# Combining the experts' outputs by adding DMAs while the last two experts run

## What is computed

```python
g_sel = argmax(g_logits); g_w = softmax(g_logits)[g_sel]
top_val, top_idx = top_k(expert logits of that group, 2)
top_w = softmax(top_val) * g_w
hid = silu(xs @ w_gate[e]) * (xs @ w_up[e])          # 1024 -> 512, per expert
x = x + sum over the 2 chosen e of top_w * (hid @ w_down[e])
```

## Time and profile before

| what | value |
|---|---|
| median of 3 runs | 1806.68 us (1804.47 to 1806.95) |
| the profiled execution | 1805.12 us |
| its span, first to last instruction | 1803.3 us |
| granted TensorE clock, mean | 0.991 |
| DMA moved | 241.31 MB |

### The profile page before, as it was taken

How to read it: one execution, slowest core, us unless ns; L and a number is a source line. 1 busy time by engine, 2 the same in 40 slices (tenths; PEclk the granted TensorE clock), 3 DMA queues, 4 the chain that set the end, 5 groups by cost and what they waited for, 6 DMA issues and landing times.

```text
span 1803.3 us, 25340 instructions
## 1 busy us (share of the span) xinstructions
PE 1745.9 (97%) x10151; PEld 1436.3 (80%) x10151; DVE 1184.1 (66%) x1701; ACT 888.6 (49%) x1413; POOL 349.9 (19%) x228
## 2 busy tenths in 40 slices
PE   9999999999999999999999999999999989999993
PEld 7998788999897677788999866765568868888882
DVE  6666645554466655555776588586764466988896
ACT  5525434234334544334344455556552366878781
POOL 4333222001242322001000276310010030000001
PEclk9999999999999999999999999999999999999997
DMA  6203112223312212333222210213243449999984
GB/s 191 77 25 100 47 48 72 93 71 117 97 59 67 65 39 71 101 94 99 94 94 72 70 48 24 71 47 95 69 151 118 142 172 394 414 407 416 398 349 175
DMA packets 121903, 241.31 MB, mean 134 GB/s; under 512 B 9577, under 2 KB 101258, under 8 KB 115642
## 3 DMA queue, kind: packets, MB, share of 16 engines
q1 hardware_dynamic: 113770, 212.81, 33.4%
q0 software_dynamic: 4464, 16.25, 2.4%
q10 hardware_dynamic: 3552, 10.62, 1.5%
HBM read 223.41 MB, written 16.25 MB: 133 GB/s over the span
## 4 chain that ended last, share of the span: by engine, by line
PE 51%; DVE 5%; ACT 4%; issue 1%; DMA 1%; POOL 0%; POOLq 0%; ACTq 0%; DVEq 0%
PE acc L1451 15%; PE acc L900 10%; PE acc L1166 9%; PE acc L1191 7%; PE acc L1255 2%; PE acc L1269 2%; PE acc L1286 1%; PE acc L1277 1%; PE acc L1151 1%; PE acc L1435 1%; DVE upad L2890 1%; DVE qk L2890 1%; ACT v L2087 1%; DMA qk<-y_rows,back_rows 0%; PE acc L1073 0%
## 5 line engine op out<-in xcount | busy, mean ns | idle before, releaser
L900 PE MATMUL acc<-h_split,ring_split 128*128 128x264 f32 (+1 forms) x864 | 269.4, 312 | 0.0
L900 PEld LDWEIGHTS acc<-h_split,ring_split 128*128 128x128 f32 x864 | 162.3, 188 | 9.7
L1191 PE MATMUL acc<-ring_split,h_split 128*128 128x256 f32 x384 | 107.9, 281 | 0.0
L900 PE MATMUL acc<-h_split,qk_split 128*128 128x264 f32 (+1 forms) x288 | 92.7, 322 | 1.3 <-DVE ring_split L2346 1.3
L900 PE MATMUL acc<-ring_split,qk_split 128*128 128x264 f32 (+1 forms) x288 | 92.2, 320 | 0.0
L3206 POOL TENSOR_TENSOR latent<-latent 128x528 f32<-128x528 f32 x18 | 29.1, 1619 | 285.7 <-ACT latent L1615 285.4
L2346 DVE TENSOR_TENSOR ring_split<-ring,qk_split 128x1024 fp32r<-128x1024 f32 (+1 forms) x56 | 59.4, 1070 | 34.1 <-ACT qk_split L1620 34.1
L900 PE MATMUL acc<-h_split,krope_split 128*128 128x264 f32 (+1 forms) x240 | 79.4, 331 | 1.9 <-POOL ring_split L3220 1.9
L3220 POOL TENSOR_TENSOR ring_split<-ring,krope_split 128x1024 fp32r<-128x1024 f32 x20 | 48.1, 2405 | 152.3 <-ACT krope_split L1620 152.3
L900 PE MATMUL acc<-ring_split,krope_split 128*128 128x264 f32 (+1 forms) x240 | 77.0, 321 | 0.0
L2346 DVE TENSOR_TENSOR ring_split<-ring,o_split 128x1024 fp32r<-128x1024 f32 (+1 forms) x32 | 43.9, 1389 | 49.3 <-ACT o_split L1620 49.1
(11 more groups left out here) (604 smaller groups left out, 5578.8 us busy)
## 6 DMA issues: line engine op xcount, KB each, us to landing
ring<-in_w_in SPq DMA_DIRECT2D x64, 1024.0 KB, 5.3
ring<-in_w_expert_gate SPq DMA_DIRECT2D x10, 2048.0 KB, 11.0
ring<-in_w_expert_up SPq DMA_DIRECT2D x10, 2048.0 KB, 9.9
ring<-in_w_expert_down SPq DMA_DIRECT2D x10, 2048.0 KB, 10.6
ring<-in_w_out SPq DMA_DIRECT2D x12, 1024.0 KB, 5.5
y_rows<-gate ACTq DMA_DIRECT2D x16, 512.0 KB, 10.4
hres<-in_w_expert_up SPq DMA_DIRECT2D x3, 2048.0 KB, 10.5
qk<-in_w_expert_down SPq DMA_DIRECT2D x3, 2048.0 KB, 11.0
```

The lines of the kernel that those rows point to most:

```text
L900: ins = nc.tensor.matmul(dst[0:rows_, half, 0:x.shape[1]], w[:, k, :], x, start=(k == 0 and i == 0), stop=(k == last and i == 2), skip_gro ...
L1191: ins = nc.tensor.matmul(dst[:, side, 0:WIDE], x[k][:, rows_], w, start=(k == 0 and part == 0), stop=(k == DC - 1 and part == 2), skip_gro ...
```

## The change

- **Weights in the eviction.** PE makes the weight of each expert's 128 slots (`slot_weights`: 8 small matmuls in iteration 0), and ACT's eviction of `y` multiplies by it as its scale. Rows of a token's two experts then only have to be added.
- **Adding gathers.** POOL gathers rows of `y_rows` with an adding DMA straight into `x_tok`: step 0 four tiles of the lower choice, after expert 13's rows are stored; step 1 four tiles of the other choice, after expert 14's. Where a token's lower choice is expert 14 the two are swapped. A token of expert 15 or past the 128 rows gets a row of zeros instead. DVE's eight multiply-adds fall away, and SP stores each tile when its two gathers have landed. The row numbers are made in the expert loop on DVE (`places_of_all`, `rows_fetched`, at e = 1 and e = 5).
- **Expert 15** is not stored in `y_rows`. Its down product is made by column halves (all of columns 0 to 511, then 512 to 1023), each evicted by itself, and POOL adds each half's 128 rows of 2 KB to `out` in HBM by an adding scatter, after the stores of `out`. Its tokens' numbers come from a pick on DVE, 4 small matmuls on PE (`rows_added`, e = 4) and two small steps on DVE.
- **Order of the last experts.** down(14) goes ahead of up(15): PE runs half of gate(15), turns the hidden part of 14, the other half of gate(15), down(14), up(15), hidden part and down of 15. ACT and DVE follow; on DVE the last weight half comes behind `hidden_low(15)`. The last three outputs have SBUF places of their own (`y_at`).
- **Overflow.** An overflow tile is weighted and added to `out` by a scatter. One block of zeros is stored instead of seven. POOL reaches the overflow count when both scatters have landed.

```diff
+ADDED = 1
+FETCHED = EXPERTS - ADDED
...
+        y_at = [y_out] * (EXPERTS - 3) + [x_gath[0], y_out, x_gath[1]]
...
-            granules += [("gate", e + 1), ("up", e + 1), ("down", e)]
+            granules += [("gate", e + 1)] + [("up", e + 1), ("down", e)][::1 if e < EXPERTS - 2 else -1]
...
+            for i in range(QT):
+                sp.wait_ge(rows_back[i], 32)
+                sp.dma_start(out[0, i * P:(i + 1) * P, :], x_tok[:, i, :]).then_inc(stored, 16)
...
+            def last_out_of_hidden(e):
+                i = granule_no["down", e]
+                hu, hl = (t.rearrange("p (k s) -> p k s", k=HID // P) for t in (ht_up, ht_low))
+                for side in range(2):
+                    n_ = slice(side * 512, side * 512 + 512)
+                    for half in range(2):
+                        pe.wait_ge(w_low_made, 2 * i + half + 1)
+                        wu, wl = granule_half(i, half, "up"), granule_half(i, half, "low")
+                        for k in range(HID // P // 2):
+                            c = half * HID // P // 2 + k
+                            ins = three(TWO["y"][:, side, :], hu[:, c, :], hl[:, c, :], wu[:, k, n_], wl[:, k, n_],
+                                        c == 0, c == HID // P - 1)
+                    done(ins, ("y_side", side) if side == 0 else ("y", e))
...
-            for e in range(EXPERTS - 1):
+            for e in range(EXPERTS - 2):
                 gate_of(e + 1)
                 hidden_of(e)
                 into_hidden("up", e + 1)
-                if e + 2 < EXPERTS:
-                    turn_expert(e + 2)
+                turn_expert(e + 2)
+                if e == 0:
+                    slot_weights()
+                if e == 4:
+                    rows_added()
                 down_of(e)
+            gate_of(EXPERTS - 1, range(1))
+            hidden_of(EXPERTS - 2)
+            into_hidden("gate", EXPERTS - 1, range(1, 2))
+            down_of(EXPERTS - 2)
+            into_hidden("up", EXPERTS - 1)
             hidden_of(EXPERTS - 1)
...
+            def last_out(side, label):
+                act.wait_ge(psum_filled, at(psum_filled, label))
+                e, n_ = EXPERTS - 1, slice(side * 512, side * 512 + 512)
+                evacuated(nc.scalar.activation(y_at[e][:, n_], acc[:, 2, side, :], ACT.Copy,
+                                               scale=R[:, R_WS + e:R_WS + e + 1]), label)
+
             def expert_out(e):
                 act.wait_ge(psum_filled, at(psum_filled, ("y", e)))
-                if e:
+                if e == 0:
+                    act.wait_ge(dve_made, at(dve_made, "slot_weights"))
+                elif e < EXPERTS - 3:
                     act.wait_ge(y_main, 16 * e)
-                evacuated(nc.scalar.activation(y_out, acc[:, 2, :, :].rearrange("p a b -> p (a b)"), ACT.Copy),
-                          ("y", e))
+                elif e == EXPERTS - 2:
+                    act.wait_ge(y_main, 16 * (EXPERTS - 3))
+                evacuated(nc.scalar.activation(y_at[e], acc[:, 2, :, :].rearrange("p a b -> p (a b)"), ACT.Copy,
+                                               scale=R[:, R_WS + e:R_WS + e + 1]), ("y", e))
                 act.wait_ge(act_evacuated, at(act_evacuated, ("y", e)))
-                act.dma_start(y_rows[e * P:(e + 1) * P, :], y_out).then_inc(y_main, 16)
+                act.dma_start(y_rows[e * P:(e + 1) * P, :], y_at[e])\
+                    .then_inc(y_main if e < EXPERTS - 3 else y_late[e - (EXPERTS - 3)], 16)
...
+            j = 2 * granule_no["gate", EXPERTS - 1]
+            expert_out(EXPERTS - 3)
+            weights_up(j + 2)
+            hidden_up(EXPERTS - 2)
+            weights_up(j + 3)
+            expert_gated(EXPERTS - 1)
+            weights_up(j + 4)
+            weights_up(j + 5)
+            expert_out(EXPERTS - 2)
+            weights_up(j + 6)
+            weights_up(j + 7)
             hidden_up(EXPERTS - 1)
-            expert_out(EXPERTS - 2)
-            expert_out(EXPERTS - 1)
-            act.sem_inc(y_stored, 1)
-            mark(y_stored)
-            act.wait_ge(y_main, 16 * EXPERTS)
+            last_out(0, ("y_side", 0))
+            last_out(1, ("y", EXPERTS - 1))
...
+            made(tt(r(R_BY, 2, 64), r(R_SEL[0], 2, 64), R[:, R_W:R_W + 64].unsqueeze(1).to_broadcast([P, 2, 64]), ALU.mult),
+                 "by_choice")
...
+            def rows_fetched():
+
+                base, ok, row = (R[:, x:x + 8] for x in (R_S, R_S + 8, R_WT))
+                own, slot = late(K_TOKEN, 1), R[:, R_SLOT:R_SLOT + 8]
+                first = late(K_FIRST, 16).unsqueeze(1).to_broadcast([P, 8, 16])
+                chain(tt(r(R_KEY, 8, 16), r(R_SEL[0], 8, 16), first, ALU.mult))
+                chain(nc.vector.tensor_reduce(base, r(R_KEY, 8, 16), AX.X, ALU.add))
+                chain(ts(ok, slot, float(P), None, ALU.is_lt))
+                chain(stt(out=ok, in0=base, scalar=float(FETCHED * P), in1=ok, op0=ALU.is_lt, op1=ALU.mult))
+                chain(stt(out=row, in0=base, scalar=-float(FETCHED * P + 1), in1=slot, op0=ALU.add, op1=ALU.add))
+                chain(ts(row, row, own, None, ALU.subtract))
+                chain(tt(row, row, ok, ALU.mult))
+                chain(ts(row, row, own, float(FETCHED * P), ALU.add, ALU.add))
+                swap, higher, lower = R[:, R_S + 8:R_S + 12], row[:, 0:4], row[:, 4:8]
+                chain(ts(swap, base[:, 4:8], float((EXPERTS - 2) * P + 1), None, ALU.is_equal))
+                chain(tt(R[:, R_S + 12:R_S + 16], lower, higher, ALU.subtract))
+                chain(tt(swap, swap, R[:, R_S + 12:R_S + 16], ALU.mult))
+                chain(tt(higher, higher, swap, ALU.add))
+                chain(tt(lower, lower, swap, ALU.subtract))
+                made(nc.vector.tensor_copy(back_rows[:, :], row), "back_rows")
...
+                if e == 0:
+                    slot_weights()
+                elif e == 1:
+                    places_of_all()
+                elif e - 2 < ADDED:
+                    added_pick(e - 2)
+                elif e == 4:
+                    added_rows_kept()
+                elif e == 5:
+                    rows_fetched()
+            j = 2 * granule_no["gate", EXPERTS - 1]
+            weights_low(j + 2)
+            hidden_low(EXPERTS - 2)
+            weights_low(j + 3)
+            weights_low(j + 4)
+            weights_low(j + 5)
+            weights_low(j + 6)
+            expert_hidden(EXPERTS - 1)
             hidden_low(EXPERTS - 1)
-
-            chain(stt(out=R[:, R_Q:R_Q + 64], in0=R[:, R_P:R_P + 64], scalar=1.0, in1=R[:, R_M:R_M + 64],
-                      op0=ALU.add, op1=ALU.mult))
-            chain(ts(R[:, R_Q:R_Q + 64], R[:, R_Q:R_Q + 64], -1.0, None, ALU.add))
-            places = r(R_Q, QT, 16)
+            weights_low(j + 7)
...
-            for i in range(QT):
-                dve.wait_ge(rows_back[i], 32)
-                for j in range(2):
-                    ins = stt(out=x_tok[:, i, :], in0=returned[:, 2 * i + j, :],
-                              scalar=R[:, R_WT + 4 * j + i:R_WT + 4 * j + i + 1], in1=x_tok[:, i, :],
-                              op0=ALU.mult, op1=ALU.add)
-                    if j == 0:
-
-                        ins.then_inc(summed, 1)
-                        dve.wait_ge(summed, i + 1)
-                ins.then_inc(combined, 1)
...
-            for k in range(OVER):
-                pool.dma_start(y_rows[(EXPERTS + k) * P:(EXPERTS + k + 1) * P, :], padf[:, 0:D])\
-                    .then_inc(y_zeroed, 16)
+            pool.dma_start(y_rows[FETCHED * P:(FETCHED + 1) * P, :], padf[:, 0:D]).then_inc(y_zeroed, 16)
...
+            pool.wait_ge(dve_made, at(dve_made, "back_rows"))
+            pool.wait_ge(act_evacuated, at(act_evacuated, ("x_tok", QT - 1)))
+            pool.wait_ge(y_zeroed, 16)
+            pool.wait_ge(y_main, 16 * (EXPERTS - 3))
+            for step, j in enumerate((1, 0)):
+                pool.wait_ge(y_late[step], 16)
+                for i in range(QT):
+                    if step:
+                        pool.wait_ge(rows_back[i], 16)
+                    nc.gpsimd.indirect_dma_start(x_tok[:, i, :], None, y_rows,
+                                                 bass.IndirectOffsetOnAxis(back_rows[:, 4 * j + i:4 * j + i + 1], 0),
+                                                 compute_op=ALU.add).then_inc(rows_back[i], 16)
...
+            pool.wait_ge(stored, 16 * QT)
+            pool.wait_ge(dve_made, at(dve_made, "added_rows"))
+            for side, label in enumerate((("y_side", 0), ("y", EXPERTS - 1))):
+                pool.wait_ge(act_evacuated, at(act_evacuated, label))
+                n_ = slice(side * 512, side * 512 + 512)
+                nc.gpsimd.indirect_dma_start(out[0].rearrange("t (a d) -> (t a) d", a=2),
+                                             bass.IndirectOffsetOnAxis(added_rows[:, side:side + 1], 0),
```

(27 more changed lines are left out.)

117 lines of the change are left out of this document (53 added, 64 removed).

## The result

The changed kernel takes 1808.80 us (median of 17 runs, 1806.62 to 1810.13); the kernel before, run beside it, 1804.65 (17 runs, 1802.33 to 1809.39). The ratio is 1.0017, with a 95% interval of [1.0011, 1.0024]: slower, by 2 to 4 us, where 1795 had been forecast. The profiled execution is the one of 1806.62, the fastest of the 17; its span is 1804.8, so 1.8 lie outside, as before. Its end stands 11.6 us behind the 1793.2 of the prediction's sum.

What follows compares the result with a forecast made beforehand. PE bounds the expert loop; 27.9 us lie behind it, mostly eight gathers waiting for all experts. Span end 1770.2 + 8.5p, at p = 2.6 1793.2, plus 1.8 outside the span: 1795; range 1789 to 1805.

Steps and rivals of the forecast that it cites:

- The loop: Expert loop: new PE and DVE steps delay everything later by 2.8 us, between 0 and 4.
- The term of 1.5 for the matmuls: Expert loop on PE: 8 + 4 small matmuls at 0.14 each, less overlap, add 1.5 us.
- The reordering: PE's tail: down 14 ends five us earlier, but PE's last matmul 1.9 later, with gaps of 0.7, 3.1 and 0.8.
- Rival 5: Expert 13's store: lands late beside weight loads (10.4), so step 0 starts late; time 1801; chance 0.04.
- The price p: Tail: time per gather adding into SBUF, taken as 2.6 us, the middle between 1.72 and 3.44; least trusted term.
- rival 2: Adding gathers: an add reads source row and old bytes, so its price doubles to 3.44; time 1801; chance 0.14.
- traffic beside the reads costs little: Tail's DMA: rate near 300 GB/s with gathers alone, past 400 with stores beside; ground for taking 2.6 per add.
- held by its reads more than by a full DMA: Plain gathers in the tail: 1.72 us each at near 300 GB/s, seemingly limited by reads, not DMA capacity.
- POOL's issue: Gathers and scatters on POOL: 0.94 us each plus 0.30 between; well over a microsecond would be a sign of being wrong.
- The end: Behind the last store: scatters issued 2.2, their landing 2.1 + 0.5p, branch on the overflow count 0.8.
- rival 3: Tail: no change, from adds at 3.5 to 4.3 or longer POOL issues; time 1802 to 1809; chance 0.14.
- rival 4: Step 1: adding gathers don't overlap, 5.0 us each, time 1814.5; decides from 3.9; chance 0.09.

Runs made afterwards that it cites:

- the fastest kernel: Kernel before with DVE's counts and row addresses spread over the loop, plain gathers in two steps, and the change's order of last experts: 1798.95, ratio 0.9967.

## Why the prediction was wrong

Point by point, by its own steps.

- **The loop** was to cost 2.8; it costs 4.1. The stall behind the row addresses (1.1 for 1.3) was right. The term of 1.5 for the matmuls was mis-sized: full-precision ones stand twice in the trace, 2.8. Part of it was hidden in the profiled run by luck: its loop began 1.0 earlier than that of the kernel before.
- **The reordering** was right: expert 14's product at 1765.7 for 1765.1; waits of 0.5, and of 0.9 + 1.5 ahead of down 15, for 0.7 and 3.1. PE's last matmul ends at 1781.5 for 1780.1, since down 15, reckoned at the old clock, takes 7.2 and not 6.4 with a granted clock of 0.51 in its first 3 us; as forecast nothing waits for it.
- **Rival 5** did not come: expert 13's rows are in time, and step 0's first issue begins at 1759.56 for 1758.3.
- **The price p.** 2.6 was taken for an add alone, and 2.58 is what adds alone take, 1.5 times a plain gather's 1.72. It was the middle of two bounds, with no row behind it, so that it came out is luck. The Trainium skill has half the rate for a collective that adds against one that copies ("Collectives: The Full Stack", section "The bandwidth ceiling: the fold count and why AG ≠ RS ≠ AR"). Against the 410 GB/s of plain stores the trace agrees (203 GB/s); against the some 300 of plain gathers, by which rival 2 applied it, it does not.
- **The step that failed first** is "traffic beside the reads costs little". That, and "held by its reads more than by a full DMA", was read from the GB/s of plain gathers; the DMA share, 0.96 with gathers alone, is not in those rows. Two terms rest on it. Expert 14's store was to take 2.64 and takes 5.81, because step 0 is in flight (2.57 without step 0): +3.2. By its own sum step 0 was to land at 1758.3 + 3.0 + 4 x 2.6 = 1771.7, behind this store's 1768.8, which its last paragraph lists as a sign of being wrong. Step 1 was to take 13.4 and takes 18.1: +4.7, of which the stores of `out` are 2.1 or more, and POOL's held issues some 0.5 (quartering DVE's parts gave that back, less than the spread of step 1); the cause of the rest, up to 2.1, stays open. The stores of step 1 are issued 3.9 apart in the mean (1779.19 to 1790.99 in three steps), the sum of one add and one store, 2.58 + 1.28; that they are paid one after the other is not shown by it, since copies, too, let the first stores go 4.0 and 4.1 apart. The prediction had seen that at p = 3.5 and more the gain is gone, but looked for that price in the add itself.
- **POOL's issue** was 0.94 in the sum. Adding makes it 1.53 to 1.59, and an issue that DVE held took up to 3.03. On the path that is +1.25 for the two scatters and some 0.5 of step 1. The forecast had named "well over a microsecond" as a sign of being wrong.
- **The end** was 3.4 for the landing and 0.8 for the branch; it is 4.0, 1.0, and 2.5 for a term that the sum did not have, POOL's DRAIN and the closing semaphores. It was invisible in the trace of before because another engine ended last.

The sum from expert 14's eviction: +0.7 at its end, +3.2 store, -0.5 release, +4.7 step 1, -0.9 last store and release, +1.25 scatters, +3.3 end, together 11.7; the spans say 11.6. The time lies at the upper edge of rival 3's 1802 to 1809, and longer issues, one of its two causes, are part of it; the other, p from 3.5 to 4.3, holds for the 3.9 between stores but not for the add itself (2.58). The mechanism of rival 4, adds one behind the other each for 5 us, is not what happened, though its sign is. What expert 15 no longer has to wait for is given back by a stage that is now bound by the DMA engines, from 1762 to 1793 with short pauses near 1774 and 1791.

## What to carry to other kernels

A transfer under other work is only free if the DMA engines have room: price it by the time for which it keeps them busy, not by its GB/s, and charge what runs beside it up to its full time. An adding DMA saves the vector engine's instructions, but takes half as long again on the DMA engines, and here DVE was idle in the tail, so plain gathers started early and added by DVE won. When a change makes another engine the last one, read what that engine does after its last work: its closing instructions were hidden before.

## What the runs showed of the hardware

- An adding gather into SBUF moves 203 GB/s with the engines fully busy (plain gathers: 301 at a DMA share of 0.96; plain stores: some 410), and POOL needs 1.53 to issue it (plain: 0.94).
- Expert 14's store, issued at 1766.85 with adding gathers in flight, moved no packet before 1770; all its packets came between 1770 and 1772.7.
- An adding scatter of 128 rows of 2 KB into HBM moves about 110 GB/s and lands 5.2 us after its issue; an overwriting one 2.8.
- POOL's issue is held until the DVE instruction on two SBUF tiles that was running is over, then takes 1.41 more (adding) or 0.82 (plain: the 2.08 at 1765.68 in the fastest kernel, where DVE's instruction ended at 1766.94). The Trainium skill has this as a port that one of the two holds for a whole instruction ("SBUF — State Buffer", section "SBUF: two separate sides"); the runs agree that the hold goes by instruction, since quartering DVE's shortened it. The other way round they show none: DVE's 2.28 from 1759.73 is not lengthened by POOL's issue from 1759.56.
- POOL's closing DRAIN takes 2.28 when begun after everything (1.95 to 2.36 over the runs); begun while POOL's DMAs are in flight it lasts until 1.15 to 1.4 behind their landing (scatters: 1804.4 for 1803.3; the gathers of the kernel before: 1798.98 for 1797.66), and the end comes 1.2 sooner.
